# A decoder-layer kernel on eight cores: a rearranged opening for tile 0 and tile 1

## What is computed

```python
proj = x @ w_in                                   # 1536 columns: xp 512 | u 512 | v 512
xp = proj[..., :512];  zg = gelu(proj[..., 512:]) # zg = u | v
# group A: 4 channel groups, trailing mean over w = 2, 4, 8, 16 positions, minus the token,
#          divided by min(t + 1, w); then a 128x128 map per group and a scale per channel
pool_out = (pooled_g @ pool_w[g]) * pool_scale
# group B: per chunk of 128 positions and head h
v = layer_norm(v, ln_g, ln_b)
sgu_out = u * (tril(w_s[h]) @ v + b_s[h])
mix = concat(pool_out, sgu_out) @ w_out
h = layer_norm(alpha * x + mix, ln1_g, ln1_b)
y = layer_norm(alpha * h + (silu(h @ w_gate) * (h @ w_up)) @ w_down, ln2_g, ln2_b)
```

## Time and profile before

| | us |
|---|---|
| median of 3 runs | 2476.28 (2474.8 to 2489.31) |
| the profiled execution, its own time | 2474.17 |
| its span, slowest core (core 6) | 2472.3 |
| spans of the 8 cores | 2467.5 to 2472.3 |
| mean granted TensorE clock | 0.991 to 0.993 |

### The profile page before, as it was taken

How to read it: one execution, slowest core, us unless ns; L and a number is a source line. 1 busy time by engine, 2 the same in 40 slices (tenths; PEclk the granted TensorE clock), 3 DMA queues, 4 the chain that set the end, 5 groups by cost and what they waited for, 6 DMA issues and landing times.

```text
span 2472.3 us, 33520 instructions; the slowest of 8 cores (2467.5 to 2472.3 us)
## 1 busy us (share of the span) xinstructions
PE 2399.0 (97%) x11192; PEld 1103.3 (45%) x11418; DVE 1497.5 (61%) x2383; ACT 401.8 (16%) x669; POOL 156.6 (6%) x289
## 2 busy tenths in 40 slices
PE   4799999999999999999999999999999999999998
PEld 2344444444444444444444444444444444444444
DVE  4662764748566475664747656475664757647464
ACT  1211221112111121111212112021110212111110
POOL 1111100000000000000000000000000000000000
PEclk9899999999999999999999999999999999999999
DMA  9779886654545565455644545555455644554553
GB/s 201 136 143 191 221 210 193 181 149 155 164 142 174 141 186 150 136 171 150 188 148 159 156 142 179 153 162 159 139 171 151 194 142 152 153 157 165 151 188 110
DMA packets 161928, 402.57 MB, mean 163 GB/s; under 512 B 67168, under 2 KB 67424, under 8 KB 159456
## 3 DMA queue, kind: packets, MB, share of 16 engines
q1 hardware_dynamic: 95904, 338.24, 41.4%
q0 software_dynamic: 10944, 48.53, 13.0%
q10 hardware_dynamic: 54912, 13.64, 3.1%
HBM read 384.40 MB, written 50.86 MB: 176 GB/s over the span
## 4 chain that ended last, share of the span: by engine, by line
PE 92%; DMA 3%; DVE 3%; issue 2%; POOL 0%; ACT 0%; DVEq 0%; POOLq 0%; ACTq 0%; SPq 0%
PE ps L583 24%; PE ps L580 24%; PE ps L674 22%; PE ps L513 9%; PE ps L416 4%; PE ps L381 4%; PE ps L486 4%; DMA sb_aT<-wpT 1%; DMA sb_ring<-w_gate_up 1%; DMA sb_ring<-w_down 1%; PE ps L464 0%; DVE sb_lnst L228 0%; DMA scr_dn<-sb_ring 0%; DVE sb_pA L440 0%; DVE sb_pB L440 0%
## 5 line engine op out<-in xcount | busy, mean ns | idle before, releaser
L580 PE MATMUL ps<-sb_hT,sb_ring 128*128 128x512 bf16 x2751 | 660.0, 379 | 7.2 <-DVE sb_t1r L471 3.1
L583 PE MATMUL ps<-sb_hT,sb_ring 128*128 128x512 bf16 x2776 | 662.4, 379 | 2.1
L674 PE MATMUL ps<-sb_ring,sb_aT 128*128 128x512 bf16 x2670 | 589.7, 379 | 4.3 <-DMA sb_ring<-w_down 1.3
L580 PEld LDWEIGHTS ps<-sb_hT,sb_ring 128*128 128x128 bf16 x2816 | 275.6, 98 | 337.0 <-issue 5.8
L583 PEld LDWEIGHTS ps<-sb_hT,sb_ring 128*128 128x128 bf16 x2816 | 275.9, 98 | 333.0 <-issue 1.4
L594 DVE SCALAR_TENSOR_TENSOR sb_silr<-sb_silr,ps 128x512 f32<-128x512 f32 x352 | 241.6, 686 | 283.3 <-ACT sb_silr L592 282.3
L674 PEld LDWEIGHTS ps<-sb_ring,sb_aT 128*128 128x128 bf16 x2728 | 266.5, 98 | 321.6 <-issue 1.8
L592 ACT ACTIVATE sb_silr<-ps 128x512 f32<-128x512 f32 x352 | 207.4, 594 | 892.3 <-PE ps L583 686.2
L687 DVE SCALAR_TENSOR_TENSOR sb_hr<-sb_hr,ps 128x512 f32<-128x512 f32 x124 | 76.9, 682 | 452.3 <-PE ps L674 452.3
L597 DVE SCALAR_TENSOR_TENSOR sb_aT<-sb_silr,ps 128x512 bf16<-128x512 f32 x352 | 242.2, 688 | 63.8 <-DVE sb_silr L594 60.9
L513 PE MATMUL ps<-sb_wout,sb_mixT 128*128 128x512 bf16 x1021 | 233.3, 382 | 6.0 <-DVE sb_mixT L495 5.9
(11 more groups left out here) (64 smaller groups left out, 970.0 us busy)
## 6 DMA issues: line engine op xcount, KB each, us to landing
sb_ring<-scr_gu SPq DMA_DIRECT2D x319, 512.0 KB, 5.3
sb_ring<-scr_dn SPq DMA_DIRECT2D x144, 512.0 KB, 3.3
sb_hr<-x SPq DMA_DIRECT2D x64, 512.0 KB, 8.2
out<-sb_hr SPq DMA_DIRECT2D x63, 512.0 KB, 3.1
sb_ring<-w_gate_up POOLq DMA_DIRECT2D x33, 512.0 KB, 10.3
sb_xT<-xT POOLq DMA_DIRECT2D x15, 1024.0 KB, 11.4
...
```

What stands on the lines that cost most here:

```text
L580: ins = t.matmul(ps[:, bg, :], lhsT=ring[:, s, 256 * k:256 * k + 128], rhs=hT[:, k, :], start=(k == 0), stop=(k == 7))
L583: ins = t.matmul(ps[:, bu, :], lhsT=ring[:, s, 256 * k + 128:256 * k + 256], rhs=hT[:, k, :], start=(k == 0), stop=(k == 7))
L674: ins = t.matmul(ps[:, bd[b], :], lhsT=aT[:, k, b * 128:(b + 1) * 128], rhs=ring[:, s, 512 * kk:512 * kk + 512], start=(k == 0), stop=(k = ...
```

## The change

The prologue puts every load on POOL's queue, in the order of use, with 32 semaphores there instead of 8: xT and wv in quarters, then pool_w, the scale, w_s, one 128x128 mask and b_s, wpT, three tiny ones, wu in halves, wout in quarters, ident, x0, x1, g1, b1, x2, x3. The pool scale is multiplied into pool_w before the fold (`scale_pool`), so the eight fold groups are plain copies, four on ACT and four on DVE. The bias is one matmul of ones with the mask product and four DVE ops. VectorE's order becomes: scale, four statistics, mask, fold copies, p of group 3, bias, four normalisations, p of the others. The fix-ups go to POOL. u of tile 0 is multiplied before s, its products come after; the first two blocks of `wout` accumulate k by k in the order in which the mixes come. Under tile 0's norms all matmuls of tile 1's p, v and u are put, with their ACT parts only; the DVE parts ("rest") and s of tile 1 go to slots 0 to 7 of tile 0, and o of tile 1 to slots 9 to 16. g2 and b2 are loaded in the down part of tile 0.

The diff, cut to its core:

```diff
+            for q in range(4):
+                load_xT(0, 2 * q, 2 * q + 2)
+                S.dma("pool", wv[:, 2 * q:2 * q + 2, :], wv_d[:, 2 * q:2 * q + 2, :], writes=[f"wv{q}"])
+            S.task("pool", lambda g: g.memset(ones[:], 1.0), writes=["ones"])
+            for g in range(4):
+                S.task("pool", lambda e, g=g: e.memset(xp[:, g, 0:16], 0.0), writes=[f"xp{g}"])
+            S.dma("pool", pw_ap.rearrange("p (g d) -> p g d", g=4), poolw_d, writes=pw_n)
+            S.dma("pool", sc_ap, scaleB_d, writes=sc_n)
+            S.dma("pool", t1r[:, 0, :].rearrange("p (h t) -> p h t", h=4), swT_d, writes=["t10"])
+            S.dma("pool", tri, triu_d, writes=["aT21"])
+            S.dma("pool", t1r[:, 1, :].rearrange("p (h t) -> p h t", h=4), bsB_d, writes=["t11"])
             S.dma("pool", wpT_sb, wpT_d, writes=[f"aT{i}" for i in range(8)])
-            S.dma("pool", aT[:, 9, :], sbB_d, writes=["aT9"])
-            S.dma("pool", wu[:], wu_d, writes=["wu"])
-            S.dma("pool", wout[:], wout_d, writes=["wout"])
+            S.dma("pool", sgT[:], sgT_d, writes=["sgT"])
+            S.dma("pool", sbT[:], sbT_d, writes=["sbT"])
+            S.dma("pool", icf[:], icf_d, writes=["icf"])
+            for q in range(2):
+                S.dma("pool", wu[:, 4 * q:4 * q + 4, :], wu_d[:, 4 * q:4 * q + 4, :], writes=[f"wu{q}"])
+            for q in (1, 0, 2, 3):
+                S.dma("pool", wout[:, 2 * q:2 * q + 2, :], wout_d[:, 2 * q:2 * q + 2, :], writes=[f"wout{q}"])
             S.dma("pool", ident[:], ident_d, writes=["ident"])
-            S.dma("sp", t1r[:, 0, :].rearrange("p (h t) -> p h t", h=4), swT_d, writes=["t10"])
-            S.dma("sp", t1r[:, 1, :].rearrange("p (h t) -> p h t", h=4), triu_d, writes=["t11"])
-            S.dma("sp", gur[:, 1, :], scaleB_d, writes=["gu1"])
-            S.dma("sp", gur[:, 0, :].rearrange("p (h t) -> p h t", h=4), bsB_d, writes=["gu0"])
-            S.dma("sp", sgT[:], sgT_d, writes=["sgT"])
-            S.dma("sp", icf[:], icf_d, writes=["icf"])
-            for gb in range(4):
-                load_x(gb, after=["wu"])
-            S.dma("sp", g1B[:], g1B_d, writes=["g1B"])
-            S.dma("sp", b1B[:], b1B_d, writes=["b1B"])
+            for gb in range(2):
+                load_x(gb, "pool")
+            S.dma("pool", g1B[:], g1B_d, writes=["g1B"])
+            S.dma("pool", b1B[:], b1B_d, writes=["b1B"])
+            for gb in range(2, 4):
+                load_x(gb, "pool")
+            S.task("act", lambda a: a.activation(out=pC[:, 0, 0:1], in_=mhalf[:], func=AF.Gelu),
+                   reads=["mhalf"], writes=["pC0"])
...
+        def u_first():
+            bks = [bank() for _ in range(4)]
+            for q in range(2):
+                for h in range(4):
+                    def f(t, q=q, h=h):
+                        for k in range(4 * q, 4 * q + 4):
+                            ins = t.matmul(ps[:, bks[h], :], lhsT=wu[:, k, h * 128:(h + 1) * 128], rhs=xT[:, k, :],
+                                           start=(k == 0), stop=(k == 7))
+                        return ins
+                    S.task("pe", f, reads=XT + [WU[q]], writes=[bn(bks[h])] if q else (),
+                           excl=() if q else [bn(bks[h])])
...
+        def mask_sgu():
+            S.task("dve", lambda v: v.tensor_tensor(out=wsT[:], in0=t1r[:, 0, :].rearrange("p (h t) -> p h t", h=4),
+                                                    in1=tri.unsqueeze(1).to_broadcast([128, 4, 128]),
+                                                    op=ALU.mult),
+                   reads=["t10", "aT21"], writes=["wsT"])
...
+            S.task("pe", lambda t: t.matmul(ps[:, b, :], lhsT=ones[:], rhs=wsT[:].rearrange("p h t -> p (h t)"),
+                                            start=True, stop=True),
+                   reads=["ones", "wsT"], excl=[bn(b)])
+            for h in range(4):
+                S.task("dve", lambda v, h=h: v.scalar_tensor_tensor(
+                    out=bias[:, h, :], in0=ps[:, b, h * 128:(h + 1) * 128], scalar=sbT[:, h:h + 1],
+                    in1=t1r[:, 1, h * 128:(h + 1) * 128], op0=ALU.mult, op1=ALU.add),
+                    reads=["sbT", "t11"], excl=[bn(b)], writes=["bias"])
+
+        def scale_pool():
+            S.task("dve", lambda v: v.tensor_tensor(out=aT[:, 8, :], in0=pw_ap, in1=sc_ap, op=ALU.mult),
+                   reads=pw_n + sc_n, writes=["aT8"])
...
-                S.task("dve", lambda v, kk=kk, b=b: v.tensor_tensor(out=wp[:, kk, :], in0=ps[:, b, :],
-                                                                    in1=gur[:, 1, :], op=ALU.mult),
-                       reads=["gu1"], excl=[bn(b)], writes=[f"wp{kk}"])
+                if kk % 2:
+                    S.task("dve", lambda v, kk=kk, b=b: v.tensor_copy(out=wp[:, kk, :], in_=ps[:, b, :]),
+                           excl=[bn(b)], writes=[f"wp{kk}"])
+                else:
+                    S.task("act", lambda a, kk=kk, b=b: a.activation(out=wp[:, kk, :], in_=ps[:, b, :], func=AF.Copy),
+                           excl=[bn(b)], writes=[f"wp{kk}"])
...
+        def out_first(pair):
+
+            bks = [[bank(), bank()] for _ in pair]
+            for i, k in enumerate(OUT_K):
+                def f(t, k=k, i=i):
+                    for b, bb in zip(pair, bks):
+                        for n_ in range(2):
+                            ins = t.matmul(ps[:, bb[n_], :], lhsT=mixT[:, k, b * 128:(b + 1) * 128],
+                                           rhs=wout[:, k, n_ * 512:(n_ + 1) * 512], start=(i == 0), stop=(i == 7))
+                    return ins
+                names = [bn(x_) for bb in bks for x_ in bb]
+                S.task("pe", f, reads=[f"mix{k}", WO[k // 2]], writes=names if i else (), excl=() if i else names)
+            for b, bb in zip(pair, bks):
+                ctx.setdefault(("o", b), {})["bk"] = tuple(bb)
...
-                    S.task("dve", lambda v, src=src: v.tensor_tensor(out=pC[:], in0=src[:, 16:32],
+                    S.task("pool", lambda v, src=src: v.tensor_tensor(out=pC[:, g, :], in0=src[:, 16:32],
                                                                      in1=icf[:, g, :], op=ALU.mult),
-                           reads=[sn, "icf"], writes=["pC"])
-                    S.task("dve", lambda v: v.tensor_tensor(out=mixT[:, g, 0:16], in0=pC[:], in1=xp[:, g, 16:32],
+                           reads=[sn, "icf"], writes=[f"pC{g}"])
+                    S.task("pool", lambda v: v.tensor_tensor(out=mixT[:, g, 0:16], in0=pC[:, g, :], in1=xp[:, g, 16:32],
                                                             op=ALU.subtract),
-                           reads=["pC", xn], writes=[f"mix{g}"])
+                           reads=[f"pC{g}", xn], writes=[f"mix{g}"])
+            c["rest"] = windows
...
                 fill[1 + 2 * b].append(it)
             m = mt + 1
             if m < NMT:
-                if mt:
+                if mt == 0:
+                    V = [ctx["v", 1, b] for b in range(4)]
+                    fill[0] += [rest(V[0]), rest(V[1])]
+                    fill[1] += [it_vn(1, 0), it_vn(1, 1), rest(V[2]), rest(V[3])]
+                    fill[2] += [it_vn(1, 2), it_vn(1, 3)]
+                    for i, g in enumerate((3, 2, 1, 0)):
+                        fill[i].append(rest(ctx["p", 1, g]))
+                    for h in range(4):
+                        fill[4 + h] += [it_s(1, h), rest(ctx["u", 1, h])]
+                    for n_, d_ in (("g2B", (g2B, g2B_d)), ("b2B", (b2B, b2B_d))):
+                        fill[NJ + 4].append((None, lambda n_=n_, d_=d_: S.dma("sp", d_[0][:], d_[1], writes=[n_]), 0))
...
-                o0 = 13 if mt else 5
+                o0 = 13 if mt else 9
...
         prologue()
         bks = v_first()
+        scale_pool()
         for b in range(4):
             run_slot([it_v(0, b, bks[b])])
-            if b:
-                run_slot([it_vn(0, b - 1)])
-        run_slot([it_vn(0, 3)])
+        mask_sgu()
         fold_pool()
+        run_slot([it_p(0, 3)])
         fold_sgu()
-        for g in (3, 2, 1, 0):
+        for b in range(4):
+            run_slot([it_vn(0, b)])
+        for g in (2, 1, 0):
             run_slot([it_p(0, g)])
+        bks = u_first()
         for h in range(4):
-            run_slot([it_s(0, h), it_u(0, h)])
+            run_slot([it_u(0, h, bks[h], early=True)])
+        run_slot([it for h in range(4) for it in (it_s(0, h), rest(ctx["u", 0, h]))])
+        load_xT(1)
         issue_to(RING)
-        S.dma("sp", g2B[:], g2B_d, writes=["g2B"])
-        S.dma("sp", b2B[:], b2B_d, writes=["b2B"])
-        for b in range(4):
-            run_slot([it_o(0, b)])
-            if b:
-                run_slot([it_on(0, b - 1)])
-        run_slot([it_v(1, 0), it_on(0, 3)])
-        run_slot([it_t(0, 0)])
-        run_slot([it_v(1, 1), it_vn(1, 0)])
-        run_slot([it_t(0, 1)])
-        run_slot([it_v(1, 2), it_vn(1, 1)])
```

(19 more changed lines are left out.)

144 lines of the change are left out of this document (85 added, 59 removed).

## The result

The changed kernel takes 2449.34 us (median), against 2476.28 us before (2477.01 over all runs of that kernel beside it): a ratio of 0.9883, with a 95% interval of 0.9866 to 0.99. The forecast was 2447 us, faster by over 1%. Seventeen of the changed kernel's twenty executions took 2447.47 to 2452.43 us, and a later set of the same kernel 2447.93 to 2448.17. The sets ran on several chips, so a difference of one or two us between two times says little by itself, and the experiments are read by their stages.

A forecast was written before the change was run, and what follows sets the result against it. TensorE is busy 97% of the span, so only its idle time and slow-clock matmuls before the first gate were on offer. First gate 31.1 us earlier, minus 2 for the ring: 2476.28 − 29 = 2447 us, range 2438 to 2463.

The forecast's parts named there:

- wpT to fold: Opening, loads up to the fold: the fold waits for wpT and starts at 29.5 us instead of 30.22.
- the cover: VectorE's scale_pool, four statistics and mask end by some 27 us, hidden before the fold starts at 29.5.
- Fold to the first pooling sum: Opening, fold start to first window sum: ends at 36.7 us, bounds 34.6 and 38.5; gain so far 8.9.
- VectorE from there to the last mix: Opening, first window sum to last mix: 20.2 us, last mix at 56.9; this loses 1.9.
- Last mix to the first norm: Opening: only four matmuls (0.86 us) and a 0.2 step remain after the last mix, reaching 58.0; gain 5.7.
- The norms: Opening, tile 0's norms without tile 1's statistics between: 24.4 us, ending at 82.4; gain 3.3.
- Norms to the first gate: Opening, tile 1's p, v, u moved under the norms: first gate at 89.0 us instead of 120.14; gain 15.2.
- The ring: Tile 0's weight-chunk loads: the queue has no idle time left, stall some 3 us instead of 1.3; 2 us lost.
- 1 (the ring takes the gain back): Tile 0's weight loads: at 0.3 us more per chunk, 26 chunks come 8 us later, time 2455; chance 0.15.
- 2 (fix-ups hold VectorE): Opening: eight fix-ups on POOL add 4 to 6 us on the path to the last mix, time 2452; chance 0.11.
- 3 (one slow queue): POOL's queue itself is slow: tile 1's xT lands at 96 us, first gate at 121, time 2480; chance 0.05.
- 4 (xT late): Tile 1's xT lands late, its p, v, u slide out from under the norms: time 2457; chance 0.05.

The follow-up runs named there:

- the run where v came 5 us late: Changed kernel with ten small constants and the rows of x moved from GpSimd's queue back to SyncE's: 2447.83 to 2448.91 us.
- The run with fillers: Changed kernel with 30 matmuls without use added between v and the fold: 2445.75 to 2446.27 us.
- the repeat: The changed kernel run and profiled once more, unedited: 2447.93 to 2448.17 us.

## Why the prediction was right, and where not

Of 26.9 us measured the forecast had 29. The mechanism was the forecast one, TensorE's idle time in the opening filled, with sizes off in three places. By its steps, on core 1 of the profiled execution:

- *wpT to fold:* 29.5 forecast, 30.90 measured. v was there near 21 instead of 19, VectorE was through with the mask at 28.1, and the cover held, as said. In the run where v came 5 us late the mask ended at 33.1, past the fold's start at 32.36, and the first gate hardly moved, so the cover was better than costed (in that run the pool scale was multiplied in at 5.3 us already, out of the way).
- *Fold to the first pooling sum:* this is the term that was mis-sized. It had 7.2 us and took 8.9. p3 was put at 2.0 us, near the upper clock, though the same paragraph had the fold run at the lower one; it took 3.57, all at the lower (granted clock 0.50). The run with fillers gave 1.95 for the fold and 1.89 for p3. On five of the eight cores the clock was up again by p3, and there the stretch took 6.9 to 7.2 us, as forecast; on three, among them the slowest, it took 8.9.
- *VectorE from there to the last mix:* 20.2 forecast, 20.3 measured. The bias operations, which no row of before showed, took 1.72 in all, inside the bounds of 0.7 and 3.0, and the fix-ups saved 2.0 where 1.6 stood.
- *Last mix to the first norm:* 1.1 and 1.3. *The norms:* 24.4 and 24.3. *Norms to the first gate:* 6.6 and 6.45 from the third norm's end. The deferred VectorE work cost 0.8 us at L552, near the nothing at which it was costed. Together the first gate is at 92.08 and not 89.0: 1.4 of it the fold's start, 1.7 the clock. Over the cores it is at 90.9; that the mean gain falls 3.1 short of 31.1 even so is because the forecast reckoned from core 6, the last to get there before (120.14, the mean 118.9).
- *The ring:* 2 us lost. In the profiled execution the mean over the cores lost 1.7, with up to 139.8 us on the slowest, 6.7 above the floor of 133.1; in the repeat the mean won 0.3, with at most 2.3 above that floor. The waits for late chunks are real, but a loss of 2 us against before is not shown: the kernel before had such waits too, on four of its eight cores.
- The end of the program was in no step, and costs 2.0: 1.6 for GpSimd's longer DRAIN, put at nothing because no step looked there.

The opening's 3.1 us too much and the end's 2.0 are what the sum missed on the profiled execution. There the means give 28.0 − 1.7 − 2.0 = 24.3; on the repeat, with less waiting in tile 0, 28.2 + 0.3 − 2.0, or 26.6 unrounded, close to the medians' 26.9. So part of the forecast's closeness is luck: the 2 us that it took off for the ring were not lost in the repeat, and stood in for the 2.0 of an end that it did not have. One reading of it is loose as well: the 18.2 us for wv are two waits together, the longer of 15.8.

The rivals: 1 (the ring takes the gain back) happens on a core now and then, with no more than 7 us. 2 (fix-ups hold VectorE) is false: one wait of 0.17 us for GpSimd on each core, and 2 us worse without the edit. The exclusion is in the trace, though: the first fix-up, 0.68 us long, ends 0.08 after the VectorE operation with two SBUF operands beside it, where VectorE does one in 0.17. The Trainium skill, SBUF — State Buffer, section Who interferes with whom, adds that the order of issue decides which of the two waits; here it was GpSimd, off the path. 3 (one slow queue) is false: tile 1's xT was there by 64.3 to 68.8 us, not 95. By the other page named there (the Trainium skill, DMA: Bandwidth & Descriptors, section Anatomy of one DMA) v's eight pieces would have landed, an estimate, at some 28 us (some 22 with the 256 KB that each lands instead of the 512 that it reads); they were used by 20.76, so the fixed part does not add up over queued loads. 4 (xT late) is true in small: xT lands some 3 us later than forecast, and TensorE waited for it on four of the eight cores, 0.3 to 1.9 us, but not on core 1; in the repeat on one core, 0.3 us.
